# x turned first in the opening, S5 tables on GpSimd, output weights of the selecting attention split early

## The reference

```python
# first block: two layers
hn = rms_norm(x, ln_attn[0]); x += moba_attention(hn, w_qkv, w_o, rel_bias)   # bias by distance
x += sq_relu_mlp(rms_norm(x, ln_mlp[0]), w_up[0], w_down[0])                 # relu(h@w_up)**2 @ w_down
hn = rms_norm(x, ln_attn[1])
proj = hn @ dsa_w_in; c_q, c_kv = rms_norm(...), rms_norm(...)               # the latent norms
x += selecting attention(c_q, c_kv, top 64 keys of each query) @ dsa_w_o
x += sq_relu_mlp(rms_norm(x, ln_mlp[1]), w_up[1], w_down[1])
# second block: RWKV-7 and S5 mixers side by side, cross attention, gated MLP,
# differential attention, cross attention, mixture of 8 experts
lam_bar = exp(lam * dt)          # S5: states turn by a fixed angle and decay at each step
_, states = associative_scan(combine, (lam_bar, bu))
```

## Time and profile before

| | |
|---|---|
| median of three runs | 2938.03 us (2933.53 to 2938.49) |
| the profiled execution | 2930.94 us |
| its span, first to last instruction | 2929.1 us |
| busy, share of the span | PE 89%, DVE 65%, ACT 52%, POOL 3% |
| granted TensorE clock, mean | 0.937 of full speed |
| chain that ended last | TensorE 31% of the span, issue 4%, ScalarE 3%, VectorE 2%; most of the rest isn't followed back |
| DMA | 566 MB, mean 193 GB/s |

### The profile page before, as it was taken

How to read it: one execution, slowest core, us unless ns; L and a number is a source line. 1 busy time by engine, 2 the same in 40 slices (tenths; PEclk the granted TensorE clock), 3 DMA queues, 4 the chain that set the end, 5 groups by cost and what they waited for, 6 DMA issues and landing times. The chain is left out here.

```text
span 2929.1 us, 37611 instructions
## 1 busy us (share of the span) xinstructions
PE 2601.7 (89%) x13581; PEld 2117.6 (72%) x13582; DVE 1915.5 (65%) x2368; ACT 1515.6 (52%) x1875; POOL 90.4 (3%) x115
## 2 busy tenths in 40 slices
PE   6889887997869698998978879998998999999998
PEld 5678765776765486887757657777887777777777
DVE  4555545796668544555455459885454889888888
ACT  3544335443221343444444347774443777777776
POOL 0000011000143000000100000000000000000000
PEclk9999988998887898999989879999998999999999
DMA  8346512455200541464414239995554899999996
GB/s 276 133 153 191 164 58 94 144 179 164 68 2 1 201 158 58 159 198 147 144 40 147 72 115 365 327 361 188 183 182 152 313 319 348 330 357 330 358 328 225
DMA packets 333583, 566.24 MB, mean 193 GB/s; under 512 B 21929, under 2 KB 126712, under 8 KB 333080
## 3 DMA queue, kind: packets, MB, share of 16 engines
q1 hardware_dynamic: 333464, 564.59, 56.9%
HBM read 561.19 MB, written 6.50 MB: 194 GB/s over the span
## 5 line engine op out<-in xcount | busy, mean ns | idle before, releaser
L1240 DVE TENSOR_TENSOR weights_split<-ring,weights_split 128x1024 fp32r<-128x1024 f32 x676 | 819.3, 1224 | 266.5 <-ACT weights_split L1235 229.2
L1315 PE MATMUL ps<-weights_split,expert_split 128*128 128x512 f32 x3864 | 914.6, 394 | 25.9 <-DVE expert_split L1411 17.7
L1235 ACT ACTIVATE weights_split<-ring 128x1024 fp32r<-128x1024 f32 x676 | 715.3, 1061 | 353.1 <-PE ps L1315 341.8
L1315 PEld LDWEIGHTS ps<-weights_split,expert_split 128*128 128x128 f32 x3864 | 722.3, 189 | 193.2 <-DVE weights_split L1240 38.2
L289 DVE TENSOR_TENSOR weights_split<-ring,weights_split 128x2048 fp32r<-128x2048 f32 x182 | 413.4, 2272 | 418.0 <-ACT weights_split L280 417.4
L280 ACT ACTIVATE weights_split<-ring 128x2048 fp32r<-128x2048 f32 x182 | 345.0, 1896 | 436.4 <-PE ps L460 259.0
L459 PE MATMUL ps<-normed_split,weights_split 128*128 128x512 f32 x1248 | 446.4, 400 | 25.5 <-PEq L342 25.1
L460 PE MATMUL ps<-normed_split,weights_split 128*128 128x256 f32 x1248 | 353.7, 283 | 0.0
L459 PEld LDWEIGHTS ps<-normed_split,weights_split 128*128 128x128 f32 x1248 | 239.6, 192 | 82.1 <-issue 27.5
L365 PE MATMUL ps<-weights_split,hidden_split 128*128 128x512 f32 x1032 | 244.4, 393 | 17.4 <-DVE weights_split L289 9.3
L460 PEld LDWEIGHTS ps<-normed_split,weights_split 128*128 128x128 f32 x1248 | 239.9, 192 | 1.4
(11 more groups left out here) (393 smaller groups left out, 2339.0 us busy)
## 6 DMA issues: line engine op xcount, KB each, us to landing
ring<-moe_w_gate SPq DMA_DIRECT2D x112, 1024.0 KB, 5.2
ring<-moe_w_up SPq DMA_DIRECT2D x112, 1024.0 KB, 5.3
ring<-moe_w_down SPq DMA_DIRECT2D x112, 1024.0 KB, 5.2
ring<-mlp_w_up SPq DMA_DIRECT2D x32, 1024.0 KB, 5.5
ring<-mlp_w_down SPq DMA_DIRECT2D x32, 1024.0 KB, 5.0
ring<-xa_w_kv SPq DMA_DIRECT2D x16, 1024.0 KB, 5.2
ring<-moba_w_qkv SPq DMA_DIRECT2D x12, 1024.0 KB, 12.2
ring<-da_w_qkv SPq DMA_DIRECT2D x12, 1024.0 KB, 5.2
```

What stands on the lines that cost most here:

```text
L1235: nc.scalar.activation(split_piece(p, 0), ring_piece(p), ACT.Copy).then_inc(high.sem, 1)
L1240: nc.vector.tensor_tensor(split_piece(p, 1), ring_piece(p), split_piece(p, 0).bitcast(F32), ALU.subtract)\
L1315: last = nc.tensor.matmul(ps[:, banks[half][tt], :], stationary(s, k, tt), split_piece(p, i)[:, kk * NW:(kk + 1) * NW], start=(opens and n ...
```

## The change

Four parts:

1. *Opening.* The first gain (16 rows) and the bias table are loaded ahead of the tiles, and TensorE turns these 16 rows alone, then x; the other parameter rows and the bias product come behind x. ScalarE and VectorE split one tile ahead of x; ScalarE splits the second behind it, VectorE in the next stage. SyncE goes on to fill the ring in this stage.
2. *Bias row.* It is written at the start of the next stage.
3. *Tables.* The doublings go to GpSimd, as one chain that starts when the first turn is made, with 42 instructions of 512 elements among them. VectorE keeps angles, first turn and coefficients. The doubled sine of the step angle is made by an addition instead of a multiplication by two.
4. *Latent norms.* ScalarE and VectorE split the first two tiles of `dsa_w_o` there.

```diff
 def mlp
-        stage(core, pe=pe, act=act, dve=dve, uses=len(order))
+        stage(core, pe=pe, act=act, dve=dve, pool=beside.tables_pool if beside else None, uses=len(order))
 def norm_stage, act
-            core.hi(e, core.taken + WS_BUFS)
+            core.hi(e, core.taken + (1 if opening else WS_BUFS))
         if opening:
             opening.act_gain(e)
         for b in range(4):
...
             last.then_inc(*freed.up())
+        if opening:
+            core.hi(e, core.taken + WS_BUFS)
 def norm_stage, dve
-            core.lo(e, core.taken + WS_BUFS)
+            core.lo(e, core.taken + (1 if opening else WS_BUFS))
...
+        if opening:
+            opening.dve_last(e)
 def norm_stage, pe
+        if opening:
+            opening.pe_last(e)
 class S5
-        if n == 7:
-            link = self.core.link
-            link(e, "dve", self.core.nc.vector.memset(self.COS[:, :, 0:1], 1.0))
-            link(e, "dve", self.core.nc.vector.memset(self.SIN[:, :, 0:1], 0.0))
-            self.double(e, 1, 0, ST)
-            self.double(e, 2, 0, ST)
...
+    def tables_pool(self, e):
+
+        g, link = self.core.nc.gpsimd, self.core.link
+        t1, t2 = self.qt
+        link(e, "pool", g.memset(self.COS[:, :, 0:1], 1.0))
+        link(e, "pool", g.memset(self.SIN[:, :, 0:1], 0.0))
+        e.wait_ge(*self.turn_made.at(1))
+        tt = lambda out, x0, x1, op: link(e, "pool", g.tensor_tensor(out, x0, x1, op))
+        q = (self.co, self.si)
+        for level in self.LEVELS:
+            count = min(ST, 512 // level)
+            for first in range(0, ST, count):
+                which = slice(first, first + count)
+                x1, x2 = (t[:, 0:count * level].rearrange("p (s n) -> p s n", n=level) for t in self.tmp)
+                qc, qs = bc(q[0][:, which], 2, level), bc(q[1][:, which], 2, level)
+                COS, SIN = self.COS[:, which, :], self.SIN[:, which, :]
+                tt(x1, COS[:, :, 0:level], qc, ALU.mult)
+                tt(x2, SIN[:, :, 0:level], qs, ALU.mult)
+                tt(COS[:, :, level:2 * level], x1, x2, ALU.subtract)
+                tt(x1, COS[:, :, 0:level], qs, ALU.mult)
+                tt(x2, SIN[:, :, 0:level], qc, ALU.mult)
+                tt(SIN[:, :, level:2 * level], x1, x2, ALU.add)
+            if level < self.LEVELS[-1]:
...
+                tt(q2[0], t1, t2, ALU.subtract)
+                tt(t1, q[0], q[1], ALU.mult)
+                tt(q2[1], t1, t1, ALU.add)
+                q = q2
 class Opening, sp
             e.dma_start(core.const[:, :], consts).then_inc(*self.const_landed.up(16))
+            e.wait_ge(*self.rows_cleared.at(1))
+            e.dma_start(*loads[0][0]).then_inc(*self.gain_landed.up(16))
+            e.dma_start(relb[:, :], w["rel_bias"]).then_inc(*self.rows_landed.up(16))
             core.held_from = WS_BUFS
             core.issue(e, WS_BUFS)
-            e.dma_start(relb[:, :], w["rel_bias"]).then_inc(*self.rows_landed.up(16))
-            e.wait_ge(*self.rows_cleared.at(1))
-            for dst, src in loads[0]:
+            for dst, src in loads[0][1:]:
                 e.dma_start(dst, src).then_inc(*self.rows_landed.up(16))
-            e.wait_ge(*extd.at(1))
-            e.dma_start(ext_dram, ext_sb[0:H, :]).then_inc(*bias_written.up(16))
+            core.held_from = 10 ** 9
+            core.issue(e, RING)
 class Opening, pe
-            e.wait_ge(self.rows_landed.sem, 16 * (1 + len(loads[0])))
+            e.wait_ge(*self.gain_landed.at(16))
+            nc.tensor.transpose(ps[:, 7, 0:16], core.rows[0:16, 0, :], c("ident")[0:16, 0:16]).then_inc(*turned.up())
+
+        def pe_last(self, e):
+            e.wait_ge(self.rows_landed.sem, 16 * len(loads[0]))
+            nc.tensor.transpose(ps[:, 5, 0:P], core.rows[:, 0, :], c("ident")).then_inc(*turned.up())
             nc.tensor.matmul(ps[0:H, 6, 0:CAUS], relb[:, :], c("onehot")[0:NBUCKET, :], start=True, stop=True)\
                 .then_inc(*turned.up())
-            nc.tensor.transpose(ps[:, 7, 0:P], core.rows[:, 0, :], c("ident")).then_inc(*turned.up())
 def read_bias
-        core.held_from = 10 ** 9
-        core.issue(e, RING)
-        e.wait_ge(*bias_written.at(0))
+        e.dma_start(ext_dram, ext_sb[0:H, :]).then_inc(*bias_written.up(16))
+        e.wait_ge(*bias_written.at(16))
         e.dma_start(rows_dram, bc(ext_dram, 1, P)).then_inc(*bias_spread.up(16))
 the stage of the latent norms
+    def dve(e):
+        gdve(e)
+        core.lo(e, core.taken + 3 + WS_BUFS)
+
     def act(e):
         gact(e)
+        core.hi(e, core.taken + 3 + WS_BUFS)
```

More of the change, by code:

```diff
@@ L2193, in __init__ @@
         sig = lambda n: Signal(core.nc, f"s5_{n}")
+        self.qt = [a(6528 + ST * i, ST) for i in range(2)]
+        self.turn_made = sig("first_turn")
         (self.saved, self.loaded, self.landed, self.ex, self.ang, self.trig, self.made, self.turned, self.kept_turned) = map(
@@ L2285, in tables_dve @@
             self.coefficients(e)
-        if n == 7:
-            link = self.core.link
-            link(e, "dve", self.core.nc.vector.memset(self.COS[:, :, 0:1], 1.0))
-            link(e, "dve", self.core.nc.vector.memset(self.SIN[:, :, 0:1], 0.0))
-            self.double(e, 1, 0, ST)
-            self.double(e, 2, 0, ST)
-        if n == 8:
-            self.double(e, 4, 0, ST)
-            self.double(e, 8, 0, ST)
-        first = 9
-        for level in self.LEVELS[4:]:
-            count = min(ST, 512 // level)
-            for group in range(ST // count):
-                for part in range(2):
-                    if n == first:
-                        self.double(e, level, group * count, count, (part,))
-                    first += 1
+    def tables_pool(self, e):
[7 more added lines that the diff above has]
+        for level in self.LEVELS:
+            count = min(ST, 512 // level)
+            for first in range(0, ST, count):
[10 more added lines that the diff above has]
+            if level < self.LEVELS[-1]:
+                q2 = (self.qc, self.qs) if q[0] is not self.qc else (self.qc2, self.qs2)
+                tt(t1, q[0], q[0], ALU.mult)
+                tt(t2, q[1], q[1], ALU.mult)
+                tt(q2[0], t1, t2, ALU.subtract)
+                tt(t1, q[0], q[1], ALU.mult)
+                tt(q2[1], t1, t1, ALU.add)
+                q = q2
     def tt(self, e, out, x0, x1, op):
@@ L2334, in first_turn @@
         tt(e, co, sh, sh, ALU.mult)
-        ts(e, co, co, -2.0, 1.0, ALU.mult, ALU.add)
+        self.core.nc.vector.tensor_scalar(co, co, -2.0, 1.0, ALU.mult, ALU.add).then_inc(*self.turn_made.up())
+        e.wait_ge(*self.turn_made.at(1))
     def coefficients(self, e):
@@ L2382, in prepare @@
             last.then_inc(*self.made.up())
-    def double(self, e, n, first, count, parts=(0, 1)):
-        tt = self.tt
-        q = self.turns
-        which = slice(first, first + count)
-        x1, x2 = (t[:, 0:count * n].rearrange("p (s n) -> p s n", n=n) for t in self.tmp)
-        qc, qs = bc(q[0][:, which], 2, n), bc(q[1][:, which], 2, n)
-        COS, SIN = self.COS[:, which, :], self.SIN[:, which, :]
-        if 0 in parts:
-            tt(e, x1, COS[:, :, 0:n], qc, ALU.mult)
-            tt(e, x2, SIN[:, :, 0:n], qs, ALU.mult)
-            tt(e, COS[:, :, n:2 * n], x1, x2, ALU.subtract)
-        if 1 in parts:
-            tt(e, x1, COS[:, :, 0:n], qs, ALU.mult)
-            tt(e, x2, SIN[:, :, 0:n], qc, ALU.mult)
-            tt(e, SIN[:, :, n:2 * n], x1, x2, ALU.add)
-        if 1 in parts and n < self.LEVELS[-1] and first + count == ST:
-            q2 = (self.qc, self.qs) if q[0] is not self.qc else (self.qc2, self.qs2)
-            tt(e, self.t1, q[0], q[0], ALU.mult)
-            tt(e, self.t2, q[1], q[1], ALU.mult)
-            tt(e, q2[0], self.t1, self.t2, ALU.subtract)
-            tt(e, self.t1, q[0], q[1], ALU.mult)
-            self.ts(e, q2[1], self.t1, 2.0, None, ALU.mult)
-            self.turns = q2
     def scan_project(self, e, p):
@@ L2614, in program @@
         x_landed, const_landed, rows_landed = sig("x_landed"), sig("constants_landed"), sig("rows_landed")
[L2615 removed]
+        rows_cleared, cols_ready, gain_landed = sig("rows_cleared"), sig("columns_ready"), sig("first_gain_landed")
         def sp(self, e):
@@ L2643, in dve_parameters, with dve_last @@
             e.wait_ge(*turned.at(1))
+            nc.vector.tensor_copy(core.cols[:, 0, 0:16], ps[:, 7, 0:16]).then_inc(*self.cols_ready.up())
+        def dve_last(self, e):
+            e.wait_ge(*turned.at(2))
+            nc.vector.tensor_copy(core.cols[:, 0, 16:P], ps[:, 5, 16:P])
+            e.wait_ge(*turned.at(3))
             nc.vector.tensor_tensor(ext_sb[0:H, :], ps[0:H, 6, 0:CAUS], c("future")[0:H, :], ALU.add)\
                 .then_inc(*extd.up())
[L2646 to L2647 removed]
         def pe(self, e):
             e.wait_ge(*self.const_landed.at(16))
[L2651 removed]
+            e.wait_ge(*self.gain_landed.at(16))
[3 more added lines that the diff above has]
```

(5 more changed lines are left out.)

3 lines of the change are left out of this document (removed).

## The result

The changed kernel takes **2919.61 us** in the median of five runs (2918.65 to 2923.11), beside 2938.03 (2927.10 to 2943.28) for the kernel before: ratio 0.9948, 95% interval 0.9925 to 0.9970. By the medians that is 18.4 us less, where 13.6 were forecast; the ratio, which here agrees with that of the means, makes it 15.3.

A forecast was written before the change was run, and what follows sets the result against it. Stages closed by five-engine barriers last as long as their last engine. Opening -4.9, latent norms with projection -4.2 and tables -4.5 sum to -13.6: 2917.3 us profiled, 2924.4 us median, range 2913 to 2933.

The forecast's parts named there:

- Opening, -4.9: First product at 24.4 instead of 29.29 us, the barrier waiting for SyncE's fifth tile; bounds -7.4 and -1.5.
- rival 3: Opening: SyncE doesn't hold it, -7.4, total about -16, chance 0.12; or it gives only 1.5, total -10, chance 0.08.
- Bias, 0: Bias row's write, spread and skewed read move behind the opening's tiles and stay hidden: cost 0, bound +3.
- Latent norms, +1.15: VectorE's two subtractions behind its norm end at 397.15, where the stage ended on ScalarE at 395.99.
- projection, -5.35: Output projection behind the selecting attention: 31.07 us becomes 25.72, as in the first layer, with the weights split beforehand.
- Tables, -12.5 + 7.7, rounded to -4.5: Second MLP: doublings off VectorE save 12.5 us, waits for GpSimd give back 7.7; bounds -12.5 and +10.
- less 0.6 is 0.45, and since a late turn isn't given back by an early one, 0.7 a period: Second MLP: three VectorE waits, 1.05 together, less slack 0.6; loss set at 0.7 us per two-tile period, 11 periods.
- GpSimd's chain: Second MLP: 75 us of GpSimd work takes 115 to 125 us beside VectorE, ending inside the stage by some 20 us.
- the reading of L2483: VectorE's 512-element L2483 takes 691 ns at best, 1034 in the median beside GpSimd: read as 0.34 us of waiting.
- the trace agrees with the turns, not with the full length: Second MLP: VectorE and GpSimd take turns, since L2483 waits half an instruction's 0.69, rather than blocking for whole instructions.
- holds VectorE up by at most 0.7: Second MLP: the longest VectorE wait for a 512-element GpSimd instruction, taken as twice 0.34 us.
- Rival 1: Second MLP: full-length turns, three waits of 0.6 each, 13 us back; tables 0 to +1, total -8.5, 2929.5; chance 0.18.

The follow-up runs named there:

- x_hold: Changed kernel with SyncE issuing the opening's fifth tile only in the next stage, behind the bias row's write; median 2916.73 us, ratio 0.9925 to the kernel before.
- x_latent: Kernel before with only the early split of the output weights in the latent norms; median 2925.18 us, ratio 0.9960.
- x_small: Changed kernel with GpSimd's long doublings cut to at most 256 elements an instruction; median 2919.67 us, ratio 0.9936 to the kernel before.

## Why the prediction was right

The sign, the place of each gain and most sizes hold; the median came out 4.8 us under the forecast. By the lengths in the two profiles the terms sum to -15.3: -4.70, +1.49, -5.34 and -6.72.

- *Opening, -4.9.* 24.4 forecast, 24.59 in after: -4.70. That SyncE's fifth tile would hold it was shown by x_hold (-3.0 when it goes), against rival 3. VectorE's end, 21.5 forecast, was at 21.20.
- *Bias, 0.* The row's write, its spread and skewed read went out at 24.55, 32.99 and 48.18; TensorE waited for none of it, nor for a late tile.
- *Latent norms, +1.15, and projection, -5.35.* +1.49 and -5.34 in the profile. The +0.34 missed are between the subtractions' end and VectorE's start in the next stage (0.76, where ScalarE's end had 0.34 behind it). TensorE starts there 0.39 behind the subtractions, as the forecast would have it, and in x_latent VectorE does too (16.22, +1.12); why VectorE comes later in after stays open. The projection's price was taken from the first layer's, which has low clock near its start itself (0.72 between 131 and 137 us in before); in seven of ten profiles the low stretch is gone with the wait, and the price is 6.9. That is the one gain the forecast left out: 1.5 us.
- *Tables, -12.5 + 7.7, rounded to -4.5.* The first number measured 12.65. The second measured 5.93, so the part gives 6.7. Mis-sized was the step "less 0.6 is 0.45, and since a late turn isn't given back by an early one, 0.7 a period": the waits on the path were rightly sized (between 558 and 672 L289 takes 2640 ns in the mean of 20, 0.35 over its 2292; the square, L554, 913 over 691; so 0.92 for the three against 1.05), but the loss was 5.93 over eleven periods, 0.54 each. 0.92 less the slack of 0.6 would be 0.32: late turns do cost more than early ones give back, but less than was allowed for them.
- *GpSimd's chain.* 115 to 125 us forecast, 125.6 measured; 512 elements take it 1.04 with a repeated input and 1.29 without, forecast 1.2.

Wrong was the reason behind the waits, and the reading of L2483 that it rests on. The 0.34 isn't what a turn shorter than a whole instruction costs; it is what was left of GpSimd's instruction each time, as the lines at 881.99 and 882.61 show. So "the trace agrees with the turns, not with the full length" was a misreading, and "holds VectorE up by at most 0.7" falls: single waits reach 1.10, and each is what GpSimd's instruction has left, less some 0.14. The Trainium skill ("SBUF — State Buffer", Who interferes with whom) says that whoever comes first has the shared ports for its whole instruction and that the other waits until it has finished. The trace agrees, as does L546 with one input in PSUM, which kept its 0.68. Rival 1 took that rule and still came out too dear (0 to +1 for the tables, measured -6.7), because it let each of the three instructions meet GpSimd every time. Where a subtraction waits in after, it waits 0.54 in the mean of thirteen, near the 0.6 that rival 1 took. But VectorE often finds GpSimd's instruction nearly done: of the 15 subtractions with a line of their own between 585 and 672, three don't wait and five wait less than 0.35. That the mean came out near the forecast's 0.35 was luck. The rule gives how long a meeting lasts; how many there are has to be counted.

The total: 14.6 ± 0.8 at equal clock, 18.4 and 21.9 by the medians of the two comparisons, 15.3 and 21 by their ratios, 13.6 forecast. The excess of the medians goes with after's higher mean clock (0.9352 against 0.9322). Removed waits explain a part of that, as shown in the projection. Whether they raise the clock elsewhere, or the runs drew a better one by chance, stays open; so do x_latent's 12 us by the ratio and x_small's 5.1 at equal clock.

## What to carry to other kernels

Before a tuned stage is given work on GpSimd, price the meetings: VectorE instructions with two SBUF inputs wait for what is left of GpSimd's, and here nearly half of the 12.65 us saved came back as 5.93 of turns, and how long GpSimd's chain becomes decides whether the barrier waits for it. When waits are taken out of an opening, look at who is last next; here it was the queue that issues DMAs, and moving one issue gave 3 us more. Shorter GpSimd instructions halve the longest wait, not the sum of the waits. And where one stretch of unchanged code varies by 15 us with the granted clock, compare stages by their own rows and whole runs at equal clock.

## What the runs showed of the hardware

- A VectorE instruction with two SBUF inputs that meets GpSimd's waits for what is left of it less 0.13 to 0.15 us, in 18 meetings of 19; the nineteenth found 0.10 left and didn't wait. A blocked GpSimd instruction of 512 elements with a repeated input ends 0.90 after VectorE's, against 1.04 alone.
- Four tiles of 1 MB were issued in 5.56 us (x_hold); in after the five issues took 0.39, 0.58, 1.46, 2.88 and 3.39 us: the issue itself lasts longer when several have been sent just before.
- The same instructions took 165 to 180 us at a mean granted clock of 0.83 to 0.75: single profiles of one kernel can't tell 5 us in such a stage.
- After a wait of 7.14 us TensorE began at half clock (1.2 of 2.4 GHz) in four profiles of four; after one of 2.27 us it fell to it in three of ten.
